# Shift and scale of sub-layer 1 in four column blocks instead of three

## The reference

```
def ada_modulation(cond, w_ada, b_ada):
    m = jax.nn.silu(cond) @ w_ada + b_ada
    return [p[:, None, :] for p in jnp.split(m, N_MOD, axis=-1)]
...
    sh1, sc1, g1, sh2, sc2, g2 = ada_modulation(cond, w_ada, b_ada)
    h = rms_norm(x, g_norm1) * (1 + sc1) + sh1
    proj = h @ w_in
...
    x = x + g1 * (mixed @ w_out)
    h2 = rms_norm(x, g_norm2) * (1 + sc2) + sh2
    x = x + g2 * ec_moe(h2, w_router, w_gate, w_up, w_down)
```

## Time and profile before

| | |
|---|---|
| median of three runs | 1526.85 us |
| span of the profiled execution | 1525.0 us |
| outside that span, to the median | 1.85 us |
| PE busy | 1446.9 us, 95% |
| DVE busy | 602.3 us, 39% |
| ACT busy | 255.1 us, 17% |
| moved from HBM | 565.02 MB, 375 GB/s over the span |
| first matmul of the projection | 52.70 us |

### The profile page before, as it was taken

The page is one execution under the profiler, slowest core; times in us unless marked ns, Lnnn a source line. Parts: engine busy times, 40 slices in busy tenths (PEclk is TensorE's granted clock), DMA queues, the critical chain, the costliest instruction groups (busy, mean ns, idle before and its releaser), DMA issues.

```text
span 1525.0 us, 18551 instructions
## 1 busy us (share of the span) xinstructions
PE 1446.9 (95%) x7856; PEld 882.0 (58%) x7856; DVE 602.3 (39%) x1019; ACT 255.1 (17%) x358; POOL 26.7 (2%) x58
## 2 busy tenths in 40 slices
PE   6999999999999999999989989999889899899998
PEld 3667788888889997435435335335335335335433
DVE  4433977978768986101301301301301301211313
ACT  4233223333233223000000000000000000000200
POOL 0000000000000000000000000000000000000000
PEclk9999999999999999999999999999999999999999
DMA  9999688777787659999999999999999999999999
GB/s 374 403 395 325 263 324 316 268 261 260 276 294 273 221 191 366 371 433 434 430 431 433 427 435 431 431 434 428 435 431 430 434 429 435 431 429 431 431 422 349
DMA packets 99263, 572.48 MB, mean 375 GB/s; under 512 B 9532, under 2 KB 54532, under 8 KB 76676
## 3 DMA queue, kind: packets, MB, share of 16 engines
q1 hardware_dynamic: 87824, 520.14, 83.5%
q0 software_dynamic: 6912, 50.33, 8.6%
q10 hardware_dynamic: 4468, 1.14, 0.3%
HBM read 565.02 MB, written 6.55 MB: 375 GB/s over the span
## 4 chain that ended last, share of the span: by engine, by line
PE 66%; DMA 24%; DVE 5%; SPq 2%; issue 2%; ACT 1%; ACTq 0%; DVEq 0%
PE psum L639 64%; DMA ring<-in_w_up 20%; DMA ring<-in_w_ada 2%; SPq L551 2%; DMA res<-in_w_ada 1%; DVE res L1618 1%; DVE w_parts L1508 1%; DMA ring<-in_w_down 1%; PE psum L649 0%; PE psum L825 0%; PE psum L1077 0%; DVE stat L1578 0%; DVE hid L1577 0%; PE psum L1047 0%; DVE mix L1581 0%
## 5 line engine op out<-in xcount | busy, mean ns | idle before, releaser
L639 PE MATMUL psum<-ring,hid 128*64 128x512 f32 x3024 | 679.9, 596 | 54.0 <-DMA ring<-in_w_up 40.2
L639 PEld LDWEIGHTS psum<-ring,hid 128*64 128x64 f32 x3024 | 240.2, 138 | 470.3 <-issue 414.3
L1944 DVE TENSOR_TENSOR hid<-psum,hid 128x512 f32<-128x512 f32 x16 | 11.1, 691 | 516.3 <-PE psum L639 516.3
L639 PE MATMUL psum<-h_parts,w_parts 128*128 128x384 f32 x1152 | 207.3, 337 | 1.3 <-DVE mix L1651 1.3
L639 PEld LDWEIGHTS psum<-h_parts,w_parts 128*128 128x128 f32 x1152 | 199.9, 188 | 5.1 <-issue 2.5
L1508 DVE TENSOR_TENSOR w_parts<-ring,w_parts 128x2048 fp32r<-128x2048 f32 x52 | 119.0, 2289 | 76.4 <-ACT w_parts L1208 76.2
L1208 ACT ACTIVATE w_parts<-ring 128x2048 fp32r<-128x2048 f32 x52 | 99.6, 1916 | 209.0 <-PE psum L639 176.9
L639 PE MATMUL psum<-w_parts,h_parts 128*128 128x512 f32 x432 | 103.9, 395 | 2.8 <-DVE w_parts L1508 1.5
L639 PE MATMUL psum<-ring,early 128*32 128x512 f32 (+4 forms) x694 | 96.4, 536 | 7.8 <-DMA ring<-in_w_ada 6.0
L639 PEld LDWEIGHTS psum<-w_parts,h_parts 128*128 128x128 f32 x432 | 79.5, 188 | 28.5 <-issue 10.3
L639 PEld LDWEIGHTS psum<-early,mix 128*128 128x128 f32 x768 | 86.6, 192 | 9.0 <-issue 9.0
(11 more groups left out here) (216 smaller groups left out, 754.0 us busy)
## 6 DMA issues: line engine op xcount, KB each, us to landing
ring<-in_w_up SPq DMA_DIRECT2D x30, 4096.0 KB, 23.2
ring<-in_w_gate SPq DMA_DIRECT2D x28, 4096.0 KB, 30.4
ring<-in_w_down SPq DMA_DIRECT2D x26, 4096.0 KB, 30.0
ring<-in_w_ada POOLq DMA_DIRECT2D x48, 1024.0 KB, 7.5
ring<-in_w_in SPq DMA_DIRECT2D x36, 1024.0 KB, 8.3
ring<-in_w_ada SPq DMA_DIRECT2D x28, 768.0 KB, 15.6
res<-in_w_ada SPq DMA_DIRECT2D x16, 1024.0 KB, 5.7
ring<-in_w_out SPq DMA_DIRECT2D x16, 1024.0 KB, 5.8
```

The source lines that it names most:

```text
L639: return nc.tensor.matmul(out, lhsT, rhs, start=start, stop=stop, skip_group_check=True)
L1944: tt(by_row, bank[1][:, :].rearrange("p (b a) -> p a b", a=4), by_row, ALU.mult).then_inc(act_ready, 1)
```

## The change

Block sizes become 640, 512, 512 and 384 columns: chunks 0 to 4, 5 to 8, 9 to 12, and 13 to 15. Every piece is one k now, so there are 64 instead of 40 (piece numbers: 0 to 15, 16 to 31, 32 to 47, 48 to 63), of 640, 512, 512 and 384 KB. The buffers per block are 8, 12, 12 and 10, with 12 landing semaphores, and when a buffer is free is worked out by overlap of the address ranges instead of being listed. A block with an odd number of chunks is turned in overlapping halves: 640 columns as two of 384, 384 columns as two of 256. The bias is added in four instructions a block instead of two. `PIECES_AT` has an entry for each t of ten ks, 30 in all, most with one or two pieces, where before there were 11 entries. The turns stand in the second of the three token tiles of the k before the block. In `h_block` the first chunk of blocks 1 to 3 is odd. Unit 7's parts are now made within block 3, and so ahead of ScalarE's seven small loads (the caches, gains and router weights).

```diff
-BLOCKS = [(0, 768), (768, 768), (1536, 512)]
-A_BUFS, B_BUFS = 8, 9
-PIECES = [(0, (k,)) for k in range(KC)] + [(1, (k,)) for k in range(KC)] + [(2, (2 * n, 2 * n + 1)) for n in range(KC // 2)]
...
-PIECES_AT = {(0, 2): [16, 17], (1, 2): [18, 19, 20], (2, 2): [21, 22], (3, 2): [23, 24, 25], (4, 2): [26, 27, 28, 29], (5, 0): [30, 31],
-             (6, 2): [32, 33], (7, 2): [34], (8, 2): [35, 36], (9, 2): [37], (10, 2): [38, 39]}
-TURN_AT = {(5, 1): 1, (11, 0): 2}
+BLOCKS = [(0, 640), (640, 512), (1152, 512), (1664, 384)]
+BLOCK_BUFS = [8, 12, 12, 10]
+PIECE_SEMS = 12
+TURNED = [-(-width // P // 2) for _, width in BLOCKS]
+PIECES = [(b, k) for b in range(len(BLOCKS)) for k in range(KC)]
...
+START_LOADS = [*range(12), "u0", *range(12, 19), "u1", *range(19, 25), "u2", *range(25, 32), "u3", *range(32, 37), "u4", *range(37, 50), "u5", *range(50, 55), "u6", *range(55, 64), "u7"]
+PIECES_AT = {(0, 0): [16], (0, 1): [17], (0, 2): [18], (1, 0): [19], (1, 1): [20], (1, 2): [21, 22], (2, 0): [23], (2, 1): [24, 25], (2, 2): [26],
+             (3, 0): [27, 28], (3, 1): [29], (3, 2): [30, 31],
...
+TURN_AT = {(4, 1): 1, (8, 1): 2, (12, 1): 3}
...
             def piece(n):
-                b, ks = PIECES[n]
...
+                b, k = PIECES[n]
+                width, part = BLOCKS[b][1], TURNED[b] * P
+                pe.wait_ge(piece_in[piece_sem(n)], piece_landed(n))
+                for j in range(4):
+                    at = j // 2 * width + j % 2 * (width - part)
+                    last = mm(bank[0][32 * j:32 * j + 32, 0:part], cond[:, k, :], piece_buf(n)[:, at:at + part], k == 0, k == KC - 1)
                 last.then_inc(w_used, 1)
...
             hi_part(0)
-            h_block(0, 3, 1)
+            h_block(0)
+            hi_part(1)
             hi_part(2)
-            hi_part(3)
-            h_block(1, 7, 4)
-            hi_part(5)
+            h_block(1, 6, 3)
+            hi_part(4)
+            h_block(2, 10, 5)
             hi_part(6)
-            h_block(2, None, None)
+            h_block(3, 14, 7)
```

More of the change, by code:

```diff
@@ L230, in build, with span @@
         start_rows = hid[:, cu_at + T:cu_at + T + BANK]
[L231 to L238, removed]
+        def span(what):
+            where, at = what
+            return {"late": 0, "hid": 10000, "seven": 20000, "parts": 30000}[where] + at
@@ new lines, in span_ap @@
+        def span_ap(what, n):
+            where, at = what
+            if where == "late":
+                return late[:, at:at + n]
+            if where == "hid":
+                return hid[:, at:at + n]
+            if where == "seven":
+                return ring[:, 7, at:at + n]
+            return ring[:, 4:7, :].rearrange("p s n -> p (s n)")[:, at:at + n]
+        piece_size = [2 * width for _, width in BLOCKS]
+        own = [col // P * T for col, _ in BLOCKS]
+        shared = {"late": [("late", 0), ("late", 1024)], "hid": [("hid", 0), ("hid", 1024)], "seven": [("seven", n * 1024) for n in range(4)]}
@@ new lines, in parts_bufs @@
+        def parts_bufs(b, n):
+            return [("parts", half + own[b] + i * 1024) for half in (0, KC * T) for i in range(n)]
+        piece_bufs = [[("parts", n * D) for n in range(6)] + [("seven", 0), ("seven", D)],
+                      shared["late"] + shared["hid"] + parts_bufs(1, 2) + shared["seven"],
+                      parts_bufs(2, 2) + shared["seven"] + shared["late"] + shared["hid"],
+                      shared["seven"] + shared["late"] + shared["hid"] + parts_bufs(3, 1)]
+        assert [len(bufs) for bufs in piece_bufs] == BLOCK_BUFS
@@ L240, in piece_buf, with piece_where, piece_sem @@
+        def piece_where(n):
+            b, k = PIECES[n]
+            return piece_bufs[b][k % BLOCK_BUFS[b]]
         def piece_buf(n):
-            b, ks = PIECES[n]
-            return piece_bufs[b][ks[0] // len(ks) % len(piece_bufs[b])]
+            return span_ap(piece_where(n), piece_size[PIECES[n][0]])
+        def piece_sem(n):
+            return n % PIECE_SEMS
         def piece_landed(n):
-            return sum((32 if PIECES[i][0] == 2 else 16) for i in range(n + 1) if PIECE_SEM[i] == PIECE_SEM[n])
+            return 16 * (n // PIECE_SEMS + 1)
@@ L247, in build, with piece_free, ends @@
+        def piece_free(n):
+            def ends(i):
+                lo = span(piece_where(i))
+                return lo, lo + piece_size[PIECES[i][0]]
+            return max([i + 1 for i in range(n) if piece_sem(i) == piece_sem(n) or ends(i)[0] < ends(n)[1] and ends(n)[0] < ends(i)[1]], default=0)
         ada_buf = [ring[:, 7, 0:D], ring[:, 7, D:2 * D]]
@@ L331, in build @@
         x_in = [sem(f"x_in{n}") for n in range(NT)]
-        piece_in = [sem(f"piece_in{n}") for n in range(B_BUFS)]
+        piece_in = [sem(f"piece_in{n}") for n in range(PIECE_SEMS)]
         w_used = sem("w_used")
@@ L434, in piece_load @@
             def piece_load(n):
-                b, ks = PIECES[n]
+                b, k = PIECES[n]
                 col, width = BLOCKS[b]
[L437 to L446, removed]
+                if piece_free(n):
+                    sp.wait_ge(w_used, piece_free(n))
+                src = ada_rows[k * P:(k + 1) * P, 0:2 * D].rearrange("p (m n) -> p m n", m=2)[:, :, col:col + width]
+                sp.dma_start(piece_buf(n).rearrange("p (m n) -> p m n", m=2), src).then_inc(piece_in[piece_sem(n)], 16)
             def unit_start(u, more=0):
@@ L1250, in hi_part, with h_odd, h_block @@
                 copy(w_part(u, 0), raw_unit(u)).then_inc(hi_ready, 1)
-            def h_block(b, first, more):
+            def h_odd(k):
+                for n, (lo, hi) in enumerate(COLS):
+                    last = nc.scalar.activation(xhatT[:, k, lo:hi], xhatT[:, k, lo:hi], ACT.Identity,
+                                                scale=gain[:, 0, k, n:n + 1], bias=mod3[:, k, n:n + 1])
+                last.then_inc(h_act, 1)
+            def h_block(b, first=None, more=None):
                 first_k, end_k = BLOCKS[b][0] // P, sum(BLOCKS[b]) // P
                 a.wait_ge(gains_ready, b + 1)
[L1255 to L1262, removed]
+                if first_k % 2:
+                    h_odd(first_k)
+                for k in range(first_k, end_k):
+                    if k % 2 == 0 and k + 1 < end_k:
+                        h_odd(k + 1)
+                    if k % 2:
+                        a.wait_ge(h_act, k // 2 + 1)
+                    else:
+                        a.wait_ge(h_dve, k // 2 + 1)
                     copy(hp[:, 0, k, :], xhatT[:, k, :]).then_inc(h_hi, 1)
@@ L1530, in h_even, with h_block @@
                 last.then_inc(h_dve, 1)
-            def h_block(b, first, more):
+            def h_block(b, first=None, more=None):
                 col, width = BLOCKS[b]
-                first_k, end_k = col // P, (col + width) // P
+                first_k, end_k, half = col // P, (col + width) // P, TURNED[b]
                 v.wait_ge(w_used, PIECE_ENDS[b])
-                copy(start_rows[:, 0:width // 2], bank[0][:, 0:width // 2]).then_inc(start_rows_out, 1)
+                copy(start_rows[:, 0:half * P], bank[0][:, 0:half * P]).then_inc(start_rows_out, 1)
```

43 lines of the change are left out of this document (19 added, 24 removed), and 2 rows, old and new, of the table PIECES_AT.

## The result

The changed kernel takes 1536.95 us (median of four runs, 1536.23 to 1538.51) against 1526.85 for the one before: ratio 1.0064, 95% interval 1.0051 to 1.0076. It is slower by 10.1 us; 9.4 were forecast. The profiled execution's span is 1535.0 us against 1525.0.

What follows compares the result with a forecast made beforehand. The experts were taken as bound by their weights, the stage before by PE, which passes delays on. Terms -3.3 + 3.5 + 6.3 + 3.9 - 1.2 + 0.2 = +9.4 us gave 1536.2 us, range 1532 to 1540.

Steps and rivals of the forecast that it cites:

- projection starts sooner: Start, block 0: smaller pieces arrive sooner, then PE's idle products set the pace; -3.3 us, bounds 0 and 5.2 gained.
- wider total of pieces: PE in the projection: 48 pieces of 256 columns replace 16 of 384 and 16 of 256; +3.5 us.
- more visits: Projection: PE leaves it for pieces and returns 30 times instead of 11; +6.3 us, bounds +2.3 and +7.7.
- starts of blocks: Before the first k of blocks 1 to 3: PE waits 1.8 us each for h; +3.9 us, bounds +3.0 and +4.8.
- unit 7: Before k 14: its parts, made ahead of ScalarE's seven loads, cut PE's wait from 1.8 to about 0.6; -1.2 us.
- turns: PE's turning of the blocks, now three of two and none of three; +0.2 us.
- The upper bound of 0.40 a visit: Projection: cost of a visit inside a k if a short one hides none of its weight loads; +7.7 us altogether.
- The cover of unit 8: Behind k 13: unit 8's high part now follows the seven issues, yet is ready 2 to 3 us before its consumer.
- switches that overlap: Rival B, projection: lone pieces hide their weights behind surrounding matmuls, visits add nothing; +3.1, 1530.0 us, chance 0.08.
- covered turns: Rival C, block starts: the three waits vanish since PE is late enough; +4.0, 1530.8 us, chance 0.06.
- a stage paced by the stream: Rival D, projection: PE's new work falls into gaps, only unit 7's 1.2 us come back; 1525.7 us, chance 0.05.
- slower small transfers: Rival E: smaller transfers run at 369 GB/s, piece 15 lands 1.3 us late; +10.7, 1537.5 us, chance 0.06.

Runs made afterwards that it cites:

- The run with lone products: Changed kernel plus four unused single identity products between projection matmuls, two of 128 columns and two of 32; span 1536.2 us in one execution.
- ten visits and early turns: Changed kernel with its 48 pieces in 10 visits instead of 30 and the turns one token tile earlier; 1525.40 us, ratio 0.9985.
- the first run: Changed kernel with the same 48 pieces behind the third token tile of ten ks, 10 visits instead of 30; 1529.62 us, ratio 1.0011.
- the second run: Changed kernel with the three turns one token tile earlier, behind the first tile of ks 4, 8 and 12; 1532.91 us, ratio 1.0037.
- the idle-product run: Changed kernel with three idle products behind each piece of block 0 instead of five; 1536.70 us, ratio 1.0064.
- the run with both mends and three idle products: Changed kernel with 10 visits, turns one token tile earlier and three idle products a piece instead of five; 1525.55 us, ratio 0.9986.

## Why the prediction was right

The time and the sign came out, and every term within 0.4 us. By the prediction's own steps, in us:

| step | forecast | measured | from |
|---|---|---|---|
| projection starts sooner | -3.3 | -2.9 | 49.80 against 52.70 |
| wider total of pieces | +3.5 | +3.5 | 0.435 each, as before; 0.65 only from the earlier trace rows |
| more visits | +6.3 | about +6.7 | what is left of the shift of 10.0 |
| starts of blocks | +3.9 | +3.6 | 3 x 1.69 - 1.5 |
| unit 7 | -1.2 | -1.1 | 145.27 - 140.44 - 4.15 = 0.7 against 1.8 |
| turns | +0.2 | (+0.2) | taken over, not measured apart |
| sum at the end of q | +9.4 | +10.0 | 151.43 against 141.46 |

**The start.** Idle products, not bytes, set the pace, as forecast: pieces 2.10 us apart, and with three products PE had to wait for the stream once, until 0.3 us after the time that the byte law gives. The forecast promised 0.4 us too much because it let piece 7 land at 26.3, and it was waited for until 26.66; piece 15, at 44.53 instead of 44.1, kept that distance.

**The visits.** The largest term and the one without a row for a lone piece. The value of the mid-k row held: 0.57 + 0.20 in the profile, 0.77 as forecast. Mis-sized was the visit at the end of a k. The forecast priced it at 0.28, which the earlier trace rows show for a k with no other visit; in a k cut in three it costs 0.33 like the others: k 1 takes 6.89 us (56.23 to 63.12), less 4.15 and four pieces of 0.435 that is 1.00 for three visits. So a k cut in three costs 0.72 more than one with a visit at its end, which are the 0.36 a visit of the run with ten visits, and ten ks cost some 0.5 more than the forecast. The upper bound of 0.40 a visit stood on no row. The run with lone products shows where the price arises.

The Trainium skill, TensorEngine Tiling (Array Packing), "Key Properties", says that changing the tiling mode drains TensorE. The trace agrees in the price, 0.34 us for a product of 32 columns against none for one of 128; a drain itself no row shows.

**The wider pieces.** No run changes the width alone. But with ten visits and early turns the terms left are -2.9 + 3.5 - 0.3 - 0.6 - 1.1 + 0.2 = -1.2 (ten visits of 0.28 against 3.1, three starts of 0.3 against 1.5), and in that profile the `w_ada` piece ahead of the stretch behind k 14 starts at 138.23 instead of 139.61, 1.4 sooner: a term of 3.5 fits to about 0.2 us.

**The starts of blocks.** Each lost 1.69 instead of the 1.8 that I took, and moving the turns by one tile returned 4.0 us.

**Unit 7.** The loss of 0.6 was right in part by luck. The forecast's own figures, 7.0 - 2.4 - 4.15, give 0.45. The chain took the 7.0, but k 13 started 2.2 us after the gain, not 2.4, and that makes 0.6; 0.7 was measured. The cover of unit 8 was larger than the 2 to 3 us forecast: its low part ends at 149.11 and PE comes to it at 155.6 (151.43 + 4.15).

**Everything behind.** A stage that PE works through without gaps and one that refills slots as PE releases them passed on 10.0 us as 10.2 and 10.0. The rivals: switches that overlap (1530.0) are refuted by the first run, covered turns by the waits in the profile and the second run, a stage paced by the stream by the absence of any wait for a transfer, slower small transfers by 397 and 393 GB/s with 640 KB pieces and under, where that rival had 369.

The Trainium skill, DMA: Bandwidth & Descriptors, "Measured", has 341 GB/s for transfers of 1 MB, issued from GpSimd. This trace has more with smaller ones, issued by SyncE with many in the queue, and the measurement decides; which of these differences matters no run shows.

What stays open: why the 2.4 us of the idle-product run reach the end only in part. In its profile 2.4 us are there at the end of q (147.17 against 149.57), 1.7 behind the wait on the VectorE sum (258.65 against 260.38), 1.8 at the gather (611.20 against 612.96) and 1.1 at the end of the span. The 0.7 us are that longer wait; the 0.7 among the experts are within what single executions of one kernel differ by (1535.04 to 1538.79 in that run).

## What to carry to other kernels

Finer blocks shorten the wait for the first result, but in a stage that one engine fills the price is counted in that engine's instructions: here 2.9 us of earlier start were paid with 3.5 us of wider pieces, some 7 of visits and 4 of block starts. Put small matmuls of another tile shape together, in few places, and put the step that starts a chain on other engines as far ahead of its consumer as its inputs allow. Before splitting, look for waits at one place: a unit made a few instructions earlier gave 1.6 us by itself.

## What the runs showed of the hardware

A float32 product with 32 stationary columns between matmuls of 128 columns cost 0.34 us above its own work, and a group of one or two pieces inside a k 0.33; a full-width product cost nothing above its own work.

A wait of 2.5 us for a transfer was followed by a spell of the low clock level (1.2 GHz, pieces at 1.51 us instead of 0.85), while one of 2.15 us in another execution was not (granted clock 1.00 from 30 to 50 us). The length of the last wait alone does not decide it: piece 7 ran at the low level (1.50 us) after 1.99 us in the changed kernel, and at the high one (0.85 us) after 2.00 us in the run with both mends and three idle products. Shortening idle work in front of a stream risked part of its gain: of 2.4 us, 1.0 were left in the execution where the clock fell.
